# Stationary weight units of a fused transformer step: sixteen start places in turn instead of one, 64 bytes in

## What is computed

```
for l in 0, 1:                                   # first block
    proj = x @ w_in[l]                           # 1024 x 8200
    y_ret = retention_and_gate(proj) @ w_proj_ret[l]      # 1024 x 1024
    y_ml  = mlstm_and_gate(proj) @ w_proj_mlstm[l]        # 1024 x 1024
    x = layer_norm(a * x + (gate_a * y_ret + gate_b * y_ml) @ w_out[l])
    gu = x @ w_gate_up[l]                        # 1024 x 5632
    x = layer_norm(a * x + (silu(gu[:, :2816]) * gu[:, 2816:]) @ w_down[l])
for l in 0, 1:                                   # second block
    proj = rms_norm(x) @ w_in_2[l]               # 1024 x 3584
    x = x + mixed_attention_and_lru(proj) @ w_out_2[l]    # 1024 x 1024
return rms_norm(x)
```

## Time and profile before

| | |
|---|---|
| median of 2 runs | 1189.19 us (1189.01 to 1189.37) |
| the profiled execution | 1189.2 us, of it 1187.4 us span |
| TensorE matmul / weight load busy | 98% / 88% of the span |
| VectorE / ScalarE busy | 62% / 48% |
| granted TensorE clock, mean | 0.998 |

### The profile page before, as it was taken

The page is one execution under the profiler, slowest core; times in us unless marked ns, Lnnn a source line. Parts: engine busy times, 40 slices in busy tenths (PEclk is TensorE's granted clock), DMA queues, the critical chain, the costliest instruction groups (busy, mean ns, idle before and its releaser), DMA issues.

```text
span 1187.4 us, 18024 instructions
## 1 busy us (share of the span) xinstructions
PE 1164.1 (98%) x7560; PEld 1041.3 (88%) x7560; DVE 737.5 (62%) x982; ACT 570.6 (48%) x656; POOL 25.9 (2%) x35
## 2 busy tenths in 40 slices
PE   6999999999999999999999999999999899999997
PEld 5978998998999988888998898899988689978995
DVE  4866655668555456685755657755554667775674
ACT  5454445534444434444444534445432466855673
POOL 0000000001000000000000000000000100000000
PEclk9999999999999999999999999999999999999999
DMA  8744545555765554644545457565556353437320
GB/s 293 261 168 156 174 146 177 188 194 169 265 191 186 175 197 141 237 153 142 177 142 192 163 194 230 195 211 183 194 196 213 124 193 128 141 128 253 130 84 35
DMA packets 129823, 211.44 MB, mean 178 GB/s; under 512 B 6480, under 2 KB 52560, under 8 KB 129616
## 3 DMA queue, kind: packets, MB, share of 16 engines
q1 hardware_dynamic: 126944, 202.96, 50.9%
q0 software_dynamic: 1744, 6.29, 1.9%
q10 hardware_dynamic: 1056, 1.05, 0.3%
HBM read 209.24 MB, written 1.05 MB: 177 GB/s over the span
## 4 chain that ended last, share of the span: by engine, by line
PE 93%; DVE 3%; ACT 3%; issue 1%; DMA 0%; POOL 0%; DVEq 0%; POOLq 0%; ACTq 0%
PE ps L432 89%; PE ps L621 1%; ACT wh L895 1%; PE ps L656 1%; PE ps L756 0%; DMA hml<-in_xT 0%; PE ps L604 0%; PE ps L563 0%; ACT sg L1058 0%; ACT xh L931 0%; DVE sg L1592 0%; DVE wl L1318 0%; PE ps L628 0%; PE ps L738 0%; DVE yl L1783 0%
## 5 line engine op out<-in xcount | busy, mean ns | idle before, releaser
L1318 DVE TENSOR_TENSOR wl<-raw,wh 128x2048 fp32r<-128x2048 f32 (+2 forms) x195 | 429.0, 2206 | 187.4 <-ACT wh L895 187.0
L895 ACT ACTIVATE wh<-raw 128x2048 fp32r<-128x2048 f32 (+2 forms) x195 | 364.1, 1874 | 180.7 <-PE ps L432 173.2
L432 PE MATMUL ps<-xh,wh 128*128 128x256 f32 (+1 forms) x1200 | 338.3, 282 | 0.0
L432 PE MATMUL ps<-xh,wl 128*128 128x256 f32 (+1 forms) x1200 | 333.0, 277 | 0.0
L432 PE MATMUL ps<-xl,wh 128*128 128x256 f32 (+1 forms) x1200 | 333.0, 277 | 0.0
L432 PEld LDWEIGHTS ps<-xh,wh 128*128 128x128 f32 (+1 forms) x1200 | 224.4, 187 | 3.7 <-issue 2.4
L432 PEld LDWEIGHTS ps<-xl,wh 128*128 128x128 f32 (+1 forms) x1200 | 224.3, 187 | 0.9
L432 PEld LDWEIGHTS ps<-xh,wl 128*128 128x128 f32 (+1 forms) x1200 | 223.9, 187 | 0.4
L432 PE MATMUL ps<-wh,xh 128*128 128x512 f32 (+1 forms) x512 | 204.9, 400 | 13.6 <-DVE wl L1318 11.3
L432 PE MATMUL ps<-wh,xl 128*128 128x512 f32 (+1 forms) x512 | 197.6, 386 | 0.0
L432 PE MATMUL ps<-wl,xh 128*128 128x512 f32 (+1 forms) x512 | 197.6, 386 | 0.0
(11 more groups left out here) (246 smaller groups left out, 1367.2 us busy)
## 6 DMA issues: line engine op xcount, KB each, us to landing
raw<-in_w_in SPq DMA_DIRECT2D x91, 1024.0 KB, 5.0
raw<-in_w_gate_up SPq DMA_DIRECT2D x88, 512.0 KB, 4.8
raw<-in_w_down SPq DMA_DIRECT2D x20, 1024.0 KB, 5.0
raw<-in_w_out SPq DMA_DIRECT2D x16, 1024.0 KB, 4.8
raw<-in_w_proj_ret SPq DMA_DIRECT2D x8, 1024.0 KB, 5.0
raw<-in_w_proj_mlstm SPq DMA_DIRECT2D x8, 1024.0 KB, 4.9
rows<-in_ln_g POOLq DMA_DIRECT2D x4, 512.0 KB, 4.1
rows<-in_ln_b POOLq DMA_DIRECT2D x4, 512.0 KB, 5.9
```

Of the source, the lines that this page charges most:

```text
L432: return pe.matmul(o, a, b, start=start, stop=False, skip_group_check=True)
L895: act.activation(stretch(wh, u, 0, m), raw[u % RAW][:, 0:m], ACT.Copy).then_inc(s_hi, 1)
L1318: dve.tensor_tensor(stretch(wl, u, a, nk * n), raw[u % RAW][:, a:nk * n], f32(stretch(wh, u, a, nk * n)), ALU.subtract).then_inc(s_lo, 1 i ...
```

## The change

A unit that had a skew of 16 floats now gets the skew `4 * (5 * turn % 16)` floats, where `turn` counts such units from 0: 0, 20, 40, 60, 16, 36, 56, 12, 32, 52, 8, 28, 48, 4, 24, 44 floats and again from 0. These are the sixteen multiples of 16 bytes below 256, each 5 or 6 times over the 88 units. A 1 is added to tell a unit with place 0 from one without a place, and taken off again where the skew is applied. The set of units is the same, and so are the buffers, their addresses, every instruction and its place in its engine's order; only start addresses in `wh` and `wl` differ, for all three engines that touch them. Units that aren't stationary stay at 0.

```
--- before.py
+++ after.py
@@ -90,13 +90,17 @@
 
     out = []
 
+    def place(skew):
+        turn = sum(u[3] > 0 for u in out)
+        return 4 * (5 * turn % 16) + 1 if skew else 0
+
     def cols(w, c0, n, skew=0):
         ks = w.shape[0] // P
         v = w.rearrange("(k p) c -> p k c", p=P)
         k0 = 0
         while k0 < ks:
             nk = ks % KU if ks % KU and k0 == ks - 3 * KU - ks % KU else KU
-            out.append((nk, n, [(v[:, k0:k0 + nk, c0:c0 + n], 0, n)], skew))
+            out.append((nk, n, [(v[:, k0:k0 + nk, c0:c0 + n], 0, n)], place(skew)))
             k0 += nk
 
     for l in range(DEPTH):
@@ -118,7 +122,7 @@
         for j in range(FF // 256):
             for k0 in range(0, 8, KU):
                 out.append((KU, 512, [(g[:, k0:k0 + KU, 256 * j:256 * j + 256], 0, 256),
-                                      (g[:, k0:k0 + KU, FF + 256 * j:FF + 256 * j + 256], 256, 256)], SKEW if j > 1 else 0))
+                                      (g[:, k0:k0 + KU, FF + 256 * j:FF + 256 * j + 256], 256, 256)], place(j > 1)))
         for c0 in (0, 512):
             cols(A["w_down"][l], c0, 512)
     for l in range(DEPTH):
@@ -359,7 +363,7 @@
             return stretch(r, u, 0, nk * n).rearrange("p (k c) -> p k c", k=nk)
 
         def stretch(r, u, a, b):
-            skew = units[u][3]
+            skew = max(units[u][3] - 1, 0)
             return r[u % RING][:, skew + a:skew + b]
 
         def sync(sp):
```

## The result

The changed kernel takes **1203.93 us** (median of 2 runs, 1203.45 to 1204.41) against 1189.19 us before: ratio 1.012, 95% interval 1.0104 to 1.0137. That is +14.7 us, where +5.8 us was forecast. The direction was right and the time lies in the range, but the size was two and a half times the forecast one.

The account below looks back on a forecast made before the run. TensorE, busy 98% of the span, was taken as the bound. Place 0 at +1.5 us plus the near places at +4.2 gave +5.7; 1187.4 + 5.7 + 1.8 = 1194.9, forecast 1195 us, range 1184 to 1206 (8 in 10).

Parts of the forecast that it names:

- What bounds the kernel: Whole kernel: TensorE is busy for 98% of the span, so time is the sum of distances between its starts.
- The sum of before: Kernel before, 4224 matmuls: 1296 at 117.8 ns and the rest at 113.34, mean 114.70 ns.
- The copies cost nothing: ScalarE's copy and VectorE's subtraction in the ring: the new places cost nothing; rows at 64 and 0 differ by 1 ns.
- Place 0 at 120.0 ns from cvg, +1.5 us: The 6 units at place 0, 288 matmuls: 120.0 ns each, as in cvg, +1.5 us.
- Place 64, -0.4 to +0.9 us: The 6 units at place 64: as before, 0 on average; -0.4 to +0.9 us if all at one pace.
- The other 14 places: 76 units, 3648 matmuls: loss falls linearly from 0 to 64, flat from 64 to 192, +4.2 us; chance 0.45.
- The address does nothing: Rival for TensorE's starts: the pace comes from the group, not the address; 1189 us, chance 0.13.
- Distance on both sides of 128: Rival for the stationary places: loss keeps falling to 0 cycles at 128, then rises; -5.4 us, 1184 us, chance 0.15.
- Only whole 64-byte steps help: Rival: places other than 64, 128, 192 (72 units) lose +10.7 to +18.3 us; 1200 to 1208 us, chance 0.22.
- Losses above 32 cycles: Rival: reads get in step; at 45 cycles in 82 units, +42 us, 1231 us; chance 0.05, shared with slower copies.
- The good pace of a stretch is broken by each change of place: Argument for whole-step rival: places changing every unit break what locks a stretch to its good pace for 17 units.
- Two paces at one place, picked at the start of a stretch: Stationary units at 64: 16 or 26.7 cycles lost per load, decided at the start of a stretch.

Follow-up runs that it names:

- experiment 11: Kernel before, with the stationary-only activations (hdh, hdl, yh, yl) starting at 64 modulo 256 and not at 0: 1193.02 us, ratio 1.0031.
- experiment 1: Kernel before, with all 88 stationary units at place 160 (SKEW 40 floats, not 16): 1210.07 us, ratio 1.0167.
- experiment 2: Kernel before, with all 88 stationary units at place 208 (SKEW 52 floats, not 16): 1197.99 us, ratio 1.0068.
- experiment 5: Kernel before, with all 88 stationary units at place 76 (SKEW 19 floats, not 16): 1183.97 us, ratio 0.9953.
- experiment 9: The changed kernel with its sixteen places in rising order, steps of 16 bytes and not 80: 1203.72 us, ratio 1.012 against the kernel before.
- experiment 10: Kernel before, stationary units kept at 64, all other units (tok, gate, cvg) given the sixteen places in turn: 1200.44 us in one run.
- experiment 8: Kernel before, with the 88 stationary units alternating between 64 and 76 bytes: 1187.41 us in one run.
- experiment 3: Kernel before, with the 88 stationary units at 36 to 96 bytes in steps of 4 bytes, in turn: 1202.45 us in one run.
- experiment 12: Kernel before, with all 88 stationary units and also the four cvg units at 76: 1183.31 us, ratio 0.9948.

## Why the prediction was right or wrong, point by point

- **What bounds the kernel: right.** The loss is in TensorE's starts; waits and the other engines didn't move.
- **The sum of before: right.** 114.70 ns was worked out from stretches, 114.77 comes from the starts of each unit. The stretch at 43.33 us that the prediction calls mqk1's is mqk0's second unit with half of one of mqk1; the count of 72 matmuls stands. "The loss is one per weight load and not one per column" holds at place 0 only: at 64 it is 16 or 26.7 cycles with 256 columns and 48 with 512 (experiment 11).
- **The copies cost nothing: right,** 1910 and 2291 ns against 1917 and 2292.
- **Place 0 at 120.0 ns from cvg, +1.5 us: right,** 119.9 ns and +1.5 us. **Place 64, -0.4 to +0.9 us: right,** +0.2 us.
- **The other 14 places: wrong, and this is the whole miss.** The step that failed is the shape, "stays as at 64 in the far half of the ring". The 33 units near 0 cost +5.3 us. That this is not far from the +4.2 forecast is partly luck, since the line is wrong there too: 48 bytes was put at 116.0 ns and has 118.8. The 43 in the far half, priced at nothing, cost +8.4 us. 128 loses 29 cycles and 160 all 32. The line from 0 to 64 was drawn through two points, and the runs show no line: 64 is a narrow good place (60 has 119.6 ns and 68 has 118.4 beside it), and nearness to 0 doesn't give the loss (112 and 160 equal 0). That the time still lay in the stated range is due to its upper part, which was there for the whole-step rival and not for this shape.
- **The rivals.** "The address does nothing" falls: one number, the start place, moved the kernel from 1184 to 1210 us (experiments 1, 2, 5) with every instruction unchanged. With it falls, for this kernel, the rule of the Trainium skill, TensorE: Matmul & The Clock Gate (Part 2, step 1), that loading the next weights takes nothing from the running matmul: here the stream loses 16 to some 50 cycles per matmul with its load, and how many depends on where the two operands start. That the last 16 belong to the load as well is not shown. "Distance on both sides of 128" falls with 128 at 118.8 ns. "Only whole 64-byte steps help", 1200 to 1208 us, had the time right, and its rule in part: in the changed kernel 64 is the only one of the sixteen with the good pace. But 128 never has it, 192 had it in one unit of experiment 9, and 76 and 88 have it. Losses above 32 cycles are real in mode "tok" (42 to 53 by place in experiment 10, 48 in experiment 11) and in mode "col" came only in single units (123 ns in one at 48).
- **A rival that the prediction doesn't name:** the edit also moves the places at which ScalarE and VectorE write the ring, and their writes could be what disturbs TensorE. The traces speak against it. In ff2 to ff10 of experiment 1 the distances are 120.4 ns on average while neither engine works and 120.0 to 120.7 while one or both write the ring; in the kernel before they are 113.3 and 113.4. In experiment 11 the ring's places stay as they were, and the pace changes.
- **The good pace of a stretch is broken by each change of place** was said in favour of the whole-step rival. It isn't so: a constant place gives what the place gave in turn (experiments 1, 2), and in experiment 8 the good pace outlives the sixteen changes between 64 and 76 from ff2's second unit to the end of ff10.
- **Two paces at one place, picked at the start of a stretch: right,** and it is where the gain lay. 64, 88, 144 and 192 showed two. 76 showed a second one, 120.0 ns, only in half a unit of the scan (experiment 3), and none in the kernels with all units at 76. 0, 160 and 208 showed only one, which is not good. I had bounded the gain of a kernel at the good pace throughout at -5.7 us; experiment 5 measured -5.7, of which the distances inside the units give 5.2.

What stays open: why these places. The losses come in steps (16, 24, 26.7, 28, 32 cycles per load at 256 columns, 32 and 48 at 512), which suggests that the two reads fall into a fixed rhythm; that is not shown, and no rule is known here that gives 76 and 88 and refuses 128. The places from 4 to 32 and from 164 to 252 were only looked at in steps of 16 bytes. In the 88 units the moving operand started at 0 in every run. Whether its own place or its distance from the stationary one makes the 512-column matmuls of experiment 10 slow, and why the 256-column ones of cvg gained, was not separated. What ahead of a stretch picks its pace is open too.

## What to carry to other kernels

When TensorE is busy all the time, divide the length of an unbroken stretch by the number of starts in it, and compare that with the column count over the clock: the difference is what each matmul with its load loses, and the start addresses of the two operands can decide it. Don't interpolate between measured addresses. A kernel that gives each tile another place is one run and shows a table, which says what places to try for all tiles; it doesn't replace those runs. The scan had 88 at 114.2 ns and 76 at 114.4, and in whole kernels 76 gained 5.7 us and 88 lost 1.3. A place can have two paces, and what ran ahead decides between them, so its best stretch is no measure. And look for the place anew for each width: here 64 helps 256 columns and hurts 512.

## What the runs showed of the hardware that was not expected

- The place of the stationary operand matters to the single 4-byte step: 113.3 ns in most units at 76, 118.3 at 72, 118.7 at 80.
- A stream of loads and matmuls has a memory: the same instructions at the same addresses run at 113.3 or 117.8 ns for 816 matmuls (ff2 to ff10 of the first layer before and in experiment 10), depending on what ran ahead of them.
- With 256 moving columns 64 is a better place for the stationary operand than 0 (16 or 26.7 cycles lost, not 32), with 512 a worse one (48, not 32). With 512 columns a moving operand off 0 was worse at every place tried (231.0 to 235.4 ns by place, not 226.7); with 256, in cvg, it was better than at 0 (116.5 ns at 76 in experiment 12, not 120).
